# First expert's rows in halves, first weight rests on GpSimd, key stores behind the rows, in a two-layer hybrid trunk

## The reference, cut to what matters

```python
probs = softmax(xf @ router_w)                 # 16 experts in 4 groups
gate, e_idx = top2_inside_best_group(probs)    # gate renormalised
y = zeros
for e in range(N_EXPERTS):                     # 16
    hid = silu(xf @ w_gate_l[e]) * (xf @ w_up_l[e])
    y = y + combine[:, e:e+1] * (hid @ w_down_l[e])
h = layer_norm(ALPHA * h + y, ln2_g, ln2_b)
```

## Time and profile before

| what | value |
|---|---|
| runs | 1026.02, 1025.71, 1021.4 us |
| median | 1025.71 us |
| profiled execution: its own time, its span | 1024.62 us, 1022.8 us |
| mean granted clock of PE | 0.964 of full speed |
| busy | PE 958.5, PEld 792.0, DVE 828.2, ACT 649.4, POOL 253.8 us |
| DMA | 278.28 MB, mean 272 GB/s |

### The profile page before, as it was taken

How to read it: one execution, slowest core, us unless ns; L and a number is a source line. 1 busy time by engine, 2 the same in 40 slices (tenths; PEclk the granted TensorE clock), 3 DMA queues, 4 the chain that set the end, 5 groups by cost and what they waited for, 6 DMA issues and landing times.

```text
span 1022.8 us, 15189 instructions
## 1 busy us (share of the span) xinstructions
PE 958.5 (94%) x5102; PEld 792.0 (77%) x5102; DVE 828.2 (81%) x1213; ACT 649.4 (63%) x910; POOL 253.8 (25%) x337
## 2 busy tenths in 40 slices
PE   4999889999999999999959999898999999999992
PEld 3998668677888888888749887686888888888882
DVE  7867656779989989899784675478999898998995
ACT  4355531068888888888644454304888888888871
POOL 1223543442111111110321235334411111111021
PEclk9999989979999999999979999799999999999996
DMA  9548821389999999998972335219999999999874
GB/s 352 189 155 254 261 93 62 137 320 389 363 373 354 368 358 365 380 366 320 236 254 65 106 127 191 83 61 340 376 386 361 372 373 358 370 368 359 317 211 110
DMA packets 118318, 278.28 MB, mean 272 GB/s; under 512 B 8771, under 2 KB 11067, under 8 KB 118238
## 3 DMA queue, kind: packets, MB, share of 16 engines
q1 hardware_dynamic: 99648, 240.40, 65.4%
q0 software_dynamic: 11040, 21.14, 7.3%
q10 hardware_dynamic: 7566, 15.96, 4.5%
HBM read 266.51 MB, written 30.37 MB: 290 GB/s over the span
## 4 chain that ended last, share of the span: by engine, by line
PE 84%; DVE 8%; issue 2%; DMA 2%; ACT 1%; POOL 1%; DVEq 0%; ACTq 0%; POOLq 0%
PE PS L983 22%; PE PS L657 12%; PE PS L988 11%; PE PS L1027 11%; PE PS L1031 6%; PE PS L835 3%; PE PS L837 3%; PE PS L836 3%; PE PS L968 2%; PE PS L1007 1%; DMA xs<-H 1%; PE PS L604 1%; DVE H L1618 1%; PE PS L748 1%; PE PS L920 1%
## 5 line engine op out<-in xcount | busy, mean ns | idle before, releaser
L1484 DVE TENSOR_TENSOR w_lo<-ring,w_hi 128x1024 fp32r<-128x1024 f32 x256 | 303.9, 1237 | 41.3 <-ACT w_hi L2015 38.6
L2015 ACT ACTIVATE w_hi<-ring 128x1024 fp32r<-128x1024 f32 x256 | 260.8, 1059 | 45.0 <-PE PS L1031 27.0
L983 PE MATMUL PS<-w_hi,x_hi 128*128 128x512 f32 x512 | 164.1, 402 | 1.5 <-ACT x_hi L1999 1.5
L988 PE MATMUL PS<-w_lo,x_hi 128*128 128x512 f32 x512 | 161.9, 397 | 0.1
L983 PE MATMUL PS<-w_hi,x_lo 128*128 128x512 f32 x512 | 160.5, 394 | 1.0 <-DVE x_lo L1474 1.0
L1491 DVE TENSOR_TENSOR w_lo<-ring,w_hi 128x1024 fp32r<-128x1024 f32 x128 | 154.3, 1220 | 4.4 <-ACT w_hi L2028 4.4
L2028 ACT ACTIVATE w_hi<-ring 128x1024 fp32r<-128x1024 f32 x128 | 135.4, 1059 | 30.3 <-PE PS L988 28.6
L983 PEld LDWEIGHTS PS<-w_hi,x_lo 128*128 128x128 f32 x512 | 96.6, 189 | 24.2 <-DVE x_lo L1474 1.5
L988 PEld LDWEIGHTS PS<-w_lo,x_hi 128*128 128x128 f32 x512 | 96.0, 188 | 23.1 <-DVE w_lo L1484 1.0
L2345 POOL DMA_INDIRECT M<-xs,idx x30 | 51.8, 1725 | 248.3 <-PE PS L968 214.7
L983 PEld LDWEIGHTS PS<-w_hi,x_hi 128*128 128x128 f32 x512 | 94.1, 189 | 22.2 <-issue 1.6
(11 more groups left out here) (270 smaller groups left out, 1624.8 us busy)
## 6 DMA issues: line engine op xcount, KB each, us to landing
ring<-in_w_gate SPq DMA_DIRECT2D x32, 2048.0 KB, 15.2
ring<-in_w_up SPq DMA_DIRECT2D x32, 2048.0 KB, 17.4
ring<-in_w_down SPq DMA_DIRECT2D x32, 2048.0 KB, 15.1
ring<-in_w_in SPq DMA_DIRECT2D x8, 2048.0 KB, 17.7
ring<-in_w_out SPq DMA_DIRECT2D x4, 2048.0 KB, 8.2
ys<-H SPq DMA_DIRECT2D x2, 3072.0 KB, 20.0
H<-ys POOLq DMA_DIRECT2D x12, 512.0 KB, 8.0
M<-in_cache_k ACTq DMA_DIRECT2D x8, 512.0 KB, 4.0
```

The lines of the kernel that those rows point to most:

```text
L983: pe.matmul(PS[:, n, :], x[:, c:c + P], w_hi[j][:, k * 512:(k + 1) * 512], start=(j == 0 and k == 0 and x is x_hi[par]), stop=False)
L988: mm = pe.matmul(PS[:, n, :], x_hi[par][:, c:c + P], lo[:, k * 512:(k + 1) * 512], start=False, stop=(j == 3 and k == 1))
L1484: dve.tensor_tensor(lo, w, w_hi[j][:, :].bitcast(F32), ALU.subtract).then_inc(up_lo, 1)
L2015: act.activation(w_hi[j][:, :], quarter(3 * par + n, j)[0], ACT.Copy).then_inc(up_hi, 1)
```

## The change

1. **Halves.** `x_hi` and `x_lo` of expert 0 are made in two halves of 128x512 (`turned_half`): ACT makes half 0 when the last tile of `first_x` has filled PSUM bank 2, DVE follows. PE's gate parts j = 0, 1 wait for half 0 alone, j = 2, 3 for half 1. On DVE the indices stand between the two halves.
2. **First rests on POOL.** The rests of the gate quarters j = 0 and 1 of expert 0 are made by POOL (`early_rest`) at the head of its `moe_round`, ahead of the gather for expert 1; PE waits for them by a semaphore of their own (`early_lo`). DVE makes only the rests from j = 2 on, and raises `up_lo` by 2 in place of the two it leaves out.
3. **Keys.** PE turns head 3 directly behind head 2, ahead of `first_x(l, last - 1)`. ACT copies head 2 ahead of the last exp of the router, writes `w_hi[0]`, copies head 3, writes `w_hi[1]` and `w_hi[2]`, makes both halves, and only then issues the three key stores.
4. **Second expert's rows midway.** `turn_x(0, 1)` moves from ahead of the four up parts of expert 0 to between the second and the third.

The core of the diff:

```diff
@@ -920,6 +922,8 @@
                                    skip_group_check=True)
+                    if n + 1 == len(tiles) and k == KT // 2 - 1:
+                        mm.then_inc(xt_half_ps, 1)
                 return mm
@@ -948,8 +952,8 @@
                 keys_turned(l, (2,))
+                keys_turned(l, (3,))
                 first_x(l, last - 1)
-                keys_turned(l, (3,))
                 rank(l, last)
@@ -969,20 +973,29 @@
-                def up_half(i, par, n, js):
+                def up_half(i, par, n, js, by_halves=False):
...
                         lo = quarter(3 * par + n, j)[1]
+                        if by_halves and j == 0:
+                            pe.wait_ge(xt_half_hi, l + 1)
+                        if by_halves and j == 2:
+                            pe.wait_ge(xt_hi, E + 1)
                         pe.wait_ge(up_hi, 8 * E + 4 * n + j + 1)
                         for x in (x_hi[par], x_lo[par]):
-                            if n == 0 and j == 0 and x is x_lo[par]:
+                            if by_halves and j == 0 and x is x_lo[par]:
+                                pe.wait_ge(xt_half_lo, l + 1)
+                            elif n == 0 and j == (2 if by_halves else 0) and x is x_lo[par]:
                                 pe.wait_ge(xt_lo, E + 1)
...
                                           start=(j == 0 and k == 0 and x is x_hi[par]), stop=False)
-                        pe.wait_ge(up_lo, 8 * E + 4 * n + j + 1)
+                        if by_halves and j < 2:
+                            pe.wait_ge(early_lo, 2 * l + j + 1)
+                        else:
+                            pe.wait_ge(up_lo, 8 * E + 4 * n + j + 1)
                         for k in range(2):
@@ -1089,10 +1102,16 @@
                     E = 16 * (rb + r)
-                    pe.wait_ge(xt_hi, E + 1)
-                    up_half(0, 0, 0, range(4))
-                    turn_x(0, 1)
-                    up_half(0, 0, 1, range(4))
+                    if not seated:
+                        pe.wait_ge(xt_hi, E + 1)
+                    up_half(0, 0, 0, range(4), by_halves=seated)
+                    if seated:
+                        up_half(0, 0, 1, range(2))
+                        turn_x(0, 1)
+                        up_half(0, 0, 1, range(2, 4))
+                    else:
+                        turn_x(0, 1)
+                        up_half(0, 0, 1, range(4))
                     pe.wait_ge(xt_hi, E + 2)
@@ -1474,6 +1493,16 @@
                                       ).then_inc(xt_lo, 1)
+                def turned_half(half):
+                    if half == 0:
+                        dve.wait_ge(xt_half_hi, l + 1)
+                    else:
+                        dve.wait_ge(xt_hi, 16 * (rb + r) + 1)
+                    c = slice(512 * half, 512 * half + 512)
+                    dve.tensor_tensor(x_lo[0][:, c], PS[:, 2 + half, :], x_hi[0][:, c].bitcast(F32), ALU.subtract
+                                      ).then_inc(xt_half_lo if half == 0 else xt_lo, 1)
@@ -1589,10 +1618,15 @@
-                split_up(0, 0, 0, range(3))
-                turned(0, 0)
                 if seated:
+                    dve.sem_inc(up_lo, 2)
+                    split_up(0, 0, 0, range(2, 3))
+                    turned_half(0)
                     partial = did(index(rb, 0, key_bank(l) + 1))
+                    turned_half(1)
+                else:
+                    split_up(0, 0, 0, range(3))
+                    turned(0, 0)
                 pair(0, True, False)
@@ -1999,6 +2033,16 @@
+                def turned_half(half):
+                    if half == 0:
+                        act.wait_ge(xt_half_ps, l + 1)
+                    else:
+                        act.wait_ge(xt_ps, E0 + 1)
+                    c = slice(512 * half, 512 * half + 512)
+                    act.activation(x_hi[0][:, c], PS[:, 2 + half, :], ACT.Copy
+                                   ).then_inc(xt_half_hi if half == 0 else xt_hi, 1)
                 def split_up(i, par, n, js):
@@ -2090,8 +2134,16 @@
-                split_up(0, 0, 0, range(3))
-                turned(0, 0)
+                if seated:
+                    split_up(0, 0, 0, range(1))
+                    k_rows(l, (3,))
+                    split_up(0, 0, 0, range(1, 3))
+                    turned_half(0)
+                    turned_half(1)
+                    k_stored(l)
+                else:
+                    split_up(0, 0, 0, range(3))
+                    turned(0, 0)
                 pair(0, True, False)
@@ -2217,11 +2269,11 @@
                     p = slice(0, TN[j])
+                    if n == last:
+                        k_rows(l, (2,))
                     act.wait_ge(lg_max, 4 * l + n + 1)
...
                                    accum_out=esum[p, j:j + 1]).then_inc(ex_done, 1)
-                k_rows(l, (2, 3))
-                k_stored(l)
                 moe_round(l, rb, 0, True)
@@ -2368,8 +2420,17 @@
+            def early_rest(l, rb, j):
+                w, lo = quarter(0, j)
+                pool.wait_ge(up_hi, 128 * rb + j + 1)
+                pool.tensor_tensor(lo, w, w_hi[j][:, :].bitcast(F32), ALU.subtract).then_inc(early_lo, 1)
             def moe_round(l, rb, r, first):
                 E0 = 16 * (rb + r)
+                if first:
+                    early_rest(l, rb, 0)
+                    early_rest(l, rb, 1)
                 pool.wait_ge(idx_ready, rb + r + 1)
```

2 lines of the change are left out of this document (added).

## The result

| | before | changed |
|---|---|---|
| median, first comparison (10 runs each) | 1021.79 us | 1031.82 us |
| lowest and highest | 1017.39, 1026.62 us | 1023.87, 1037.08 us |
| ratio, 95% interval | | 1.0072 [1.0043, 1.0101] |
| median, second comparison (35 and 12 runs) | 1023.88 us | 1029.35 us |
| ratio, 95% interval | | 1.0059 [1.0033, 1.0086] |

What follows compares the result with a forecast made beforehand. It took PE's work, stands and low clock as the bound (84% of the chain of waits). 3.4 + 1.5 - 1.0 + 2.8 + 2.4 = +9.1 us on 1024.62 gave 1033.7, called 1034 us; range 1028 to 1040.

Steps and rivals of the forecast that it cites:

- Layer 1 to the second rest: Layer 1, first gate parts: PE waits for POOL's late rests, part 1's last pair starts at 713.9, not 710.53: +3.4 us.
- The second stand of 1 to 2 us: Layer 1, ahead of part 1's last pair: PE idle again for POOL's second rest, 1 to 2 us after a 5 us stand.
- Clock: Layer 1: PE's clock falls in the 5 us stand, 3 us of low clock remain behind it: +1.5 us, bounds 0 and +3.5.
- Gather: Layer 1: PE reaches the turning two parts later, so its stand for expert 1's gathered rows goes: -1.0 us.
- Midway turning: Turning to `turn_hid`: a chain of 8.2 us outlasts PE's 5.4 and 5.8 us of work: +2.8 us layer 1, +2.4 layer 0.
- Layer 0, rests on POOL: Layer 0: rests done at 216.9, before the pair at 218.87 under PE's lower clock, so they cost nothing.
- early rows: Rival: key stores held the rows up; landing 4.3 us earlier in layer 1 gives 1028.8 us, not slower; chance 0.10.
- A low clock that lasts: Rival: layer 1's low clock lasts as in layer 0, +3.5 in place of +1.5, 1036 to 1039 us; chance 0.17.
- that case: Rival: the clock stays up in layer 0, no more than 2.0 us come back, 1031.7 us; chance 0.13.
- The 2.55 us of stands for `x_hi` and `x_lo`: Layer 1: halves and later key stores would win 1.5 + 1.05 us, but the wait for POOL's rests swallows it.

Runs made afterwards that it cites:

- Run 3: The kernel before with only the first two rests moved to POOL, behind its wait for the rows in DRAM: 1.0047 of the kernel before.
- Runs 2 and 4: The kernel before with only the midway turning: 1.0046 of the kernel before; the changed kernel without its midway turning: 1.0039.
- run 7: The changed kernel with ACT's silu of expert 0 ahead of expert 1's `x_hi`: 1.0038 of the kernel before.
- run 8: The changed kernel with DVE making rests 0 and 1 between the `x_lo` halves, silu ahead of expert 1's `x_hi`: 0.9975 and 0.9996 of before.
- Run 5: The changed kernel with the first three rests on DVE again, ahead of the halves of `x_lo`: 1.0047 of the kernel before.
- run 6: The changed kernel with POOL's two first rests ahead of its wait for the rows in DRAM: 1.011 of the kernel before.

## Why the prediction was right

The sign and the size of the total came out (+9.1 us forecast; +7.4 and +6.0 measured, and both medians, 1031.8 and 1029.4 us, inside 1028 to 1040), and most of its steps can be read off stamp by stamp.

**Layer 1 to the second rest.** Forecast +3.4 us for the pair of part 1 at 710.53. Counted from the index products: 710.53 - 704.31 = 6.22 us before, 707.68 - 698.12 = 9.56 us after, **+3.3 us**. The parts of it: rows 1.1 us earlier (1.0 taken, a value chosen between nothing and the 2.2 us of evenly shared queues, so that it fits this well is in part luck; nor did the stores leave the rows' way altogether: they were issued from 698.33 to 699.80, still 2.5 us and more ahead of the landing at 702.3), rests of 2.34 us (2.6 taken, between the nearest rows; the Trainium skill's page "GPSIMD Engine Reference", section on performance versus the Vector engine, led to the estimate 2.25, which was nearer), stand of 4.84 and 4.73 us in the two profiles (5.0). The second stand of 1 to 2 us did not come: the matmuls at half clock took its place, for the same end. Run 3 has this step alone: +4.8 us, with a clock that fell ahead of it and a longer stand for the gather.

**Clock.** The step that was too large: +1.5 us taken, about +0.6 measured. From that pair to the turning there were 6.63 us for 26 matmuls that take 6.05 at full clock (12 of them take 2.79, from 711.52 to 714.31 by the stamps). The clock fell, as argued, but 2.8 of its 6.8 us lay inside the stand and 2.7 of the rest ahead of 707.7, where the second rest, ready at 707.24, would have held PE most of that time anyway. Behind that pair 1.3 us were left in place of the 3 taken.

**Gather.** -1.0 us forecast, and the stand is gone in layer 1 in both profiles.

**Midway turning.** Forecast 8.2 us from the turning's end to `turn_hid`; measured 8.1 (723.44 - 714.31 - 1.03) and 8.2 (229.26 - 220.00 - 1.04). From turning to turning it was 9.29 us before for six parts, 9.13 after for four, whose work is 2.8 us less: **+2.6 us** (2.8 taken). In layer 0 9.59 and 9.26: **+2.5 us** (2.4 taken). The stands fell where they were said to fall, on ACT in front of expert 1's first part and on DVE in front of its rests. DVE's two rests took 3.50 us there beside POOL's work (3.2 taken). Runs 2 and 4 move this step alone, +4.7 and -2.0 to -3.4 us, around the forecast of 5.2 less the gather's 1.0; run 7 takes out the link of table load and silu.

**Layer 0, rests on POOL.** Forecast nothing, the low clock covers them. In both profiles of the change there is no stand between `first_x` and the turning, but both had the low clock there. Without it the rests' effect in layer 0 is not shown.

Together the stamps give 3.3 + 0.6 - 1.0 + 2.6 + 2.5 = +8.0 us, against +7.4 and +6.0 by the ratios. The two stretches from the router are 6.5 us longer in the profile, because layer 0 had 2.8 us less of low clock than before in it, worth 1.4. Of the difference between 8.0 and the forecast of 9.1 nearly all is the clock term.

The rivals: early rows would have needed a landing 4.3 us earlier, it was 1.1. A low clock that lasts did not come in layer 1 (6.8 us, mostly hidden). In layer 0 the profiled execution had 6.8 us of low clock, the second profile 9.7, so the stretch varies from run to run and did not vanish; that case was no property of the change. The 2.55 us of stands for `x_hi` and `x_lo`, said to be swallowed by the wait for POOL, are won once the rests are elsewhere (run 8).

Run 5 gained 1.2 to 2.6 us on the change by the ratios, and 2.6 to 3.9 from the router; its own +3.9 from the router agrees with its +4.8 (interval 1.7 to 7.9 us). What stays open: whether run 8 is faster than the kernel before at all, and what its halves and its key order are worth apart. The spread of one kernel's runs, 7 to 15 us, is wider than either.

## What to carry to other kernels

Before work is handed to an idle engine, look at what that engine is waiting for at that place: here its rests stood behind a DMA wait that they did not need, and when they were put ahead of it they held the other engine's critical chain instead. Before a step is moved to hide one wait, measure the chain that hangs on it and the work that lies beside that chain; with 8.2 us of each there is no room to move it by two parts. A long stand can pull PE's clock down, and part of that price is hidden in the stand itself: count only what runs slow after the next wait would have ended. And begin the stretch that you measure ahead of everything that the edit moves.

## What was unexpected of the hardware

**How much a tiny DVE instruction can pay for POOL.** That the two engines can hold each other is a rule of the page named under run 6. What these runs add is the size. In layer 0 each of POOL's two rests held one small DVE instruction, 2.19 and 2.09 us. In layer 1 one instruction of 128x4 waited for both, 4.97 us; why it did not get in behind the first is not shown. The TENSOR_REDUCE at 208.78 kept its 0.14 us beside the second rest. So a held instruction waited out what was left of POOL's, whatever its own size. It goes the other way too, in the changed kernel: a POOL instruction of 128x2, 0.20 us elsewhere, beside a rest on DVE that had started first:

```profile
712.82 1.25 DVE L1513 TENSOR_TENSOR w_lo<-ring,w_hi 128x1024 fp32r<-128x1024 f32 x1 [0.17 <-ACT w_hi L2059]
```

```profile
713.07 1.05 POOL L2410 TENSOR_TENSOR N<-N 128x2 f32<-128x2 f32 x1
```

**The time follows the clock's low stretches.** Over a whole execution they summed to 60.5 us in the profile of the change at 1023.98 us and to 74.3 us in its second at 1029.0 us, although both have the same stands in the passage. In the profile of before they summed to 73.7 us. Outside the two stretches from the router, the change's first profile had some 13 us less of it than before's, worth 6.6 us, and that is what hides its +6.5 us. So a profiled execution alone can hide a loss of 6 us.
